# Layer norms of a two-layer hybrid decoder: who sums tiles 5 and 6 of the second token half, and where TensorE's sums stand

## What is computed

```
x <- LN(alpha*x + 0.5*SwiGLU_1(x))
p  = x @ W_in            (attention, short convolution and S5 branches, gates)
x <- LN(alpha*x + W_o( sum_i sigmoid(g_i) * y_i ))
x <- LN(alpha*x + 0.5*SwiGLU_2(x))

LN: mu = mean(x), var = mean((x - mu)^2) over the 1024 features of a token,
    y = (x - mu) / sqrt(var + eps) * g + b
```

## Time and profile before

| | us |
|---|---|
| median of 3 runs | 2511.76 |
| lowest and highest | 2508.62, 2515.42 |
| the profiled execution | 2513.35 |
| its span, first to last instruction | 2511.5 |
| TensorE busy in it | 2488.8 |
| VectorE busy | 1498.5 |
| ScalarE busy | 1056.1 |
| GpSimd busy | 1336.6 |
| mean granted TensorE clock | 0.995 |

### The profile page before, as it was taken

One profiled execution on the slowest core, in us unless ns is written; L12 is line 12 of the kernel. 1 busy time (PEld: TensorE's weight loads), 2 busy tenths in 40 slices (PEclk: granted clock), 3 DMA queues, 4 the chain that ended last, 5 costly groups with the idle time before them and its releaser, 6 DMA issues.

```text
span 2511.5 us, 50783 instructions
## 1 busy us (share of the span) xinstructions
PE 2488.8 (99%) x19996; PEld 2373.0 (94%) x19996; DVE 1498.5 (60%) x2640; ACT 1056.1 (42%) x1934; POOL 1336.6 (53%) x840
## 2 busy tenths in 40 slices
PE   9999999999999999999999999999999999999998
PEld 9999999998899999999999999999977788989897
DVE  7556956975453474535575569569754535836366
ACT  3555234235432253636354542342355322537363
POOL 4767435522244456858557674355222444669582
PEclk9999999999999999999999999999999999999999
DMA  5524323432233323333234242234222333334232
GB/s 146 135 67 106 93 77 94 112 81 66 59 81 89 101 76 101 102 101 107 79 90 135 68 114 85 76 94 112 79 68 58 82 99 97 85 101 118 84 102 84
DMA packets 479750, 232.60 MB, mean 93 GB/s; under 512 B 58960, under 2 KB 479056, under 8 KB 479536
## 3 DMA queue, kind: packets, MB, share of 16 engines
q1 hardware_dynamic: 460288, 220.53, 32.9%
q10 hardware_dynamic: 19248, 9.08, 1.5%
HBM read 220.79 MB, written 4.26 MB: 90 GB/s over the span
## 4 chain that ended last, share of the span: by engine, by line
PE 93%; issue 2%; DVE 2%; POOL 1%; ACT 1%; DMA 1%; ACTq 0%; POOLq 0%; SPq 0%; DVEq 0%
PE ps L760 54%; PE ps L928 24%; PE ps L907 4%; PE ps L785 4%; PE ps L1252 1%; PE ps L1291 1%; POOL w_lo L680 1%; PE ps L833 1%; PE ps L1256 1%; PE ps L1267 1%; PE ps L1174 0%; PE ps L1164 0%; PE ps L1269 0%; PE ps L1101 0%; PE ps L1073 0%
## 5 line engine op out<-in xcount | busy, mean ns | idle before, releaser
L680 POOL TENSOR_TENSOR w_lo<-w_raw,w_hi 128x1024 fp32r<-128x1024 f32 (+3 forms) x348 | 732.1, 2113 | 891.4 <-ACT w_hi L1423 891.0
L1423 ACT ACTIVATE w_hi<-w_raw 128x1024 fp32r<-128x1024 f32 (+3 forms) x348 | 315.6, 911 | 548.1 <-PE ps L760 227.3
L760 PE MATMUL ps<-x_hi,w_hi 128*128 128x264 f32 (+2 forms) x1904 | 288.9, 301 | 0.2
L760 PE MATMUL ps<-x_hi,w_lo 128*128 128x264 f32 (+2 forms) x1904 | 280.0, 296 | 0.6 <-POOL w_lo L680 0.6
L760 PE MATMUL ps<-x_lo,w_hi 128*128 128x264 f32 (+2 forms) x1904 | 280.3, 296 | 0.0
L760 PEld LDWEIGHTS ps<-x_hi,w_hi 128*128 128x128 f32 x1904 | 252.2, 188 | 13.5 <-ACT w_hi L1423 0.6
L680 POOL TENSOR_TENSOR w_lo<-w_pair,w_hi 128x512 fp32r<-128x512 f32 x186 | 246.6, 1340 | 30.9 <-ACT w_hi L1423 30.9
L760 PEld LDWEIGHTS ps<-x_hi,w_lo 128*128 128x128 f32 x1904 | 252.4, 188 | 10.3 <-POOL w_lo L680 1.3
L760 PEld LDWEIGHTS ps<-x_lo,w_hi 128*128 128x128 f32 x1904 | 252.5, 188 | 9.0
L680 POOL TENSOR_TENSOR w_lo<-w_sum,w_hi 128x512 fp32r<-128x512 f32 x155 | 202.6, 1320 | 93.5 <-ACT w_hi L1423 92.0
L760 PE MATMUL ps<-hid_hi,w_hi 128*128 128x264 f32 (+1 forms) x1040 | 161.9, 300 | 0.0
(11 more groups left out here) (349 smaller groups left out, 4912.2 us busy)
## 6 DMA issues: line engine op xcount, KB each, us to landing
w_raw<-in_w_in SPq DMA_DIRECT2D x82, 512.0 KB, 3.9
w_pair<-in_ffn_w_gate SPq DMA_DIRECT2D x64, 512.0 KB, 5.2
w_raw<-in_ffn_w_down SPq DMA_DIRECT2D x64, 512.0 KB, 4.1
w_pair<-in_ffn_w_up SPq DMA_DIRECT2D x60, 512.0 KB, 5.3
w_raw<-in_ffn_w_up SPq DMA_DIRECT2D x28, 512.0 KB, 3.9
w_raw<-in_ffn_w_gate SPq DMA_DIRECT2D x24, 512.0 KB, 3.8
w_raw<-in_ffn_w_down SPq DMA_DIRECT2D x32, 384.0 KB, 3.5
w_raw<-in_w_o SPq DMA_DIRECT2D x16, 512.0 KB, 4.0
```

What stands on the lines that cost most here:

```text
L680: pool.tensor_tensor(held(w_lo, c), src, held(w_hi, c).bitcast(f32), ALU.subtract).then_inc(w_split, 1)
L760: ins = nc.tensor.matmul(dst, wk, x[:, k0 + k, tokens], start=first and k == 0 and n == 0, stop=last and k == n_tiles - 1 and n == 2)
L1423: return nc.scalar.activation(out, in_, f, **kw)
```

## The change

VectorE now adds tiles 5 and 6 of the second half, and their squares, to its running totals: four additions of 128x264 more in each norm. TensorE's sums are those of the total of tiles 0 to 6 (`second_sums`) and of tile 7 (`last_sums`): 12 products, 24 rows, in each norm. In `first_products` nothing stands ahead of chunk 0 any more; the total's sums stand ahead of tile 3, tile 7's ahead of tile 5 (before: tile 7's ahead of tile 4). In the first and the fourth norm, four products of `ones` by `ones` (`keep_busy`) stand between chunk 0 and chunk 1; their output is not used.

```diff
-SUMS_AT = 4
+SUMS_AT = (3, 5)
+FILLER = 4
...
+            def keep_busy(n):
+
+                for _ in range(n):
+                    nc.tensor.matmul(ps[:, 0, 384:384 + P], ones[:], ones[:], start=False, stop=True, skip_group_check=True)
...
-                         between={(0, 0): lambda: second_sums(n, 4, 5), (0, 1): lambda: second_sums(n, 6),
-                                  (SUMS_AT, 0): lambda: second_sums(n, 7)} if n >= 0 else {})
+                         between={(0, 1): lambda: keep_busy(0 if n % 3 else FILLER), (SUMS_AT[0], 0): lambda: second_sums(n),
+                                  (SUMS_AT[1], 0): lambda: last_sums(n)} if n >= 0 else {})
...
-            def second_sums(n, *tiles):
-
-                for k in tiles:
-                    if k == WHOLE:
-                        pe.wait_ge(ln_sums, n * 3 + 4)
-                        token_sums(n, 1, stat[:, 1], 5, True, False)
-                        token_sums(n, 1, stat[:, 2], 7, True, False)
-                        continue
-                    pe.wait_ge(z_half[1], n * 4 + (k + 1))
-                    ins = token_sums(n, 1, z[:, k], 5, False, k == KD - 1)
-                    if k == KD - 1:
-                        ins.then_inc(ln_stat, 1)
-                    pe.wait_ge(ln_square, n * 12 + (k + 5))
-                    ins = token_sums(n, 1, stat[:, square_row(k, 1)], 7, False, k == KD - 1)
-                    if k == KD - 1:
-                        ins.then_inc(ln_stat, 1)
+            def second_sums(n):
+
+                pe.wait_ge(ln_sums, n * 3 + 4)
+                for src, bank in ((stat[:, 1], 5), (stat[:, 2], 7)):
+                    token_sums(n, 1, src, bank, True, False)
+
+            def last_sums(n):
+
+                k = KD - 1
+                pe.wait_ge(z_half[1], n * 4 + (k + 1))
+                token_sums(n, 1, z[:, k], 5, False, True).then_inc(ln_stat, 1)
+                pe.wait_ge(ln_square, n * 12 + (k + 5))
+                token_sums(n, 1, stat[:, 3 + k % 2], 7, False, True).then_inc(ln_stat, 1)
...
-                    if h and k > WHOLE:
+                    if h and k == KD - 1:
                         return
                     total = ps[:, 4 + h, 0:sp.half]
-                    st.done(tt(stat[:, 1, cols] if h or k == KD - 1 else total, total, z[:, k, cols], ADD))
+                    st.done(tt(stat[:, 1, cols] if k == KD - 1 - h else total, total, z[:, k, cols], ADD))
...
                         if h == 0 and k == 0:
-                            add_half_square(WHOLE, 1, 9).then_inc(ln_sums, 1)
+                            st.done(add_half_square(WHOLE, 1, 9))
...
                         if h == 0 and k in TAKES_IN[nk]:
+                            if TAKES_IN[nk][k] == 6:
+                                st.done(add_half_square(5, 1, 10))
                             take_half(TAKES_IN[nk][k], 1)
+                            if TAKES_IN[nk][k] == 7:
+                                add_half_square(6, 1, 11).then_inc(ln_sums, 1)
```

More of the change, by code:

```diff
@@ L439, in edge @@
             return ps[0:EDGE, bank, c0:c0 + min(QT[j][1], 32)]
-        def square_row(k, h):
-            return 0 if (k, h) == (KD - 1, 1) else 3 + k % 2
         def restored(l, which):
@@ L1414, in _ @@
                 ffn(l, 1)
-            second_sums(3 * DEPTH - 1, *range(WHOLE, KD))
+            second_sums(3 * DEPTH - 1)
+            last_sums(3 * DEPTH - 1)
             spread_mean(3 * DEPTH - 1, 1)
@@ L1473, in square @@
                 else:
-                    ins = ACTV(stat[:, square_row(k, h), cols], z[:, k, cols], ACT.Square)
+                    ins = ACTV(stat[:, 3 + k % 2, cols], z[:, k, cols], ACT.Square)
                 ins.then_inc(ln_square, 1)
@@ L1936, in add_half_square @@
                     dve.wait_ge(ln_square, n * 12 + square)
-                    return tt(stat[:, 2, cols] if h or k == KD - 1 else total, total, stat[:, 3 + k % 2, cols], ADD)
+                    return tt(stat[:, 2, cols] if k == KD - 1 - h else total, total, stat[:, 3 + k % 2, cols], ADD)
                 if which == 1:
@@ L2599, in _ @@
                 st.close()
-DVE_STEPS = 396
+DVE_STEPS = 408
 _WEIGHTS = ("ffn1_w_gate", "ffn1_w_up", "ffn1_w_down", "w_in", "mla_w_uq", "mla_w_ukv", "mla_w_o", "conv_w_out",
```

## The result

The changed kernel takes 2531.32 us in the median (2528.66 to 2534.3, 4 runs) against 2512.61 for the one before on the same chip (2508.62 to 2515.42, 4 runs). The ratio is 1.0077, with a 95% interval of 1.006 to 1.0094: **slower by 0.77%**, 18.7 us. The profiled execution took 2533.53 us.

A forecast was written before the change was run, and what follows sets the result against it. TensorE, busy 99%, was taken to bound the kernel, with chunk 1 gated by VectorE. 2507.1 (without clock losses) + 2.6 + 1.7 + 2.2 + 0.2 = 2513.8, plus 14.0 for three clock falls, gave 2527.8 us; range 2511 to 2532.

The forecast's parts named there:

- Chunk 1 is gated by VectorE, and the gate moves back: Chunk 1 waits for VectorE's taking of tile 7; three additions ahead delay it 0.9 us, and TensorE stands still 2.6 us.
- Second and third norm, +1.3 each at full clock: nk = 8 norms: 0.4 us from the later gate and 0.89 of sums now behind it; 2.6 us for two.
- the gate's 0.4: Second and third norm: chunk 1 starts at 902.45 where it started at 902.05.
- Fifth norm, +1.7: The gate binds already, so the whole 0.9 us delay counts, and about 0.8 of sums.
- First and fourth norm, +1.1 each: nk = 6 norms: filler 0.88 us, waits of 1.05 ahead of tile 2 and 0.6 ahead of tile 6; 2.2 for two.
- Last norm, +0.2: Additions lie in VectorE's 1.04 us wait for the last sums and TensorE has fewer sums; bounds -0.5 and +1.
- The clock, three falls at 4.66, 14.0: Second, third and fifth norm: a thinner stretch ahead of chunk 1 drops the clock in each, 4.66 us apiece, 14.0 together.
- the upper price: 4.66 us per fall rather than 1.57, since two groups of sums (total, tile 7) still lie behind the gate.
- No fall in the first and the fourth norm: The filler's 0.88 us of dense products and shorter waits keep the clock up; already in the 2507.1 baseline.
- The rival in which the clock holds: The clock holds despite the gap, 2513.8 us, or falls cost only 1.57 each, 2518.5; chance 0.28 together.
- The faster rival: VectorE's additions vanish in its waits, tile 7 is taken by 899.8 in the second norm, 2500.0 us; chance 0.08.

The follow-up runs named there:

- e1: Changed kernel with eight dense filler products between chunk 0 and chunk 1 in the second, third, fifth and last norm too; 2517.05 us, ratio 1.0023.
- e3: Changed kernel without VectorE's four additions, so TensorE's new order alone (tiles 5 and 6 missing from the second half's sums); 2520.34 us, ratio 1.0034.
- e6: Changed kernel without its own filler in the first and fourth norm (FILLER = 0); 2526.07 us, ratio 1.0063.
- e9: Changed kernel with eight one-column filler products between chunk 0 and chunk 1 in the second, third, fifth and last norm; 2529.78 us, ratio 1.0078.
- e12: Changed kernel with chunk 0's products of tiles 3 and 4 moved ahead of chunk 1 in the nk = 8 norms (lead 5); 2515.02 us, ratio 1.0013.
- e5: Kernel before with four stand-in additions more on VectorE in each norm, both inputs in SBUF; 2521.08 us, ratio 1.0043.
- e7: Kernel before with lead 4 and its sums spread among the products, tile 6's sums kept ahead of chunk 1; 2506.67 us, ratio 0.9987.
- e11: Kernel before with lead 4, sums spread (tile 6's behind chunk 1's tile 1), and four stand-in additions per norm, one input in PSUM; 2528.66 us, ratio 1.0073.
- e8: Kernel before with lead 4, sums spread (tile 6's behind chunk 1's tile 1), and four stand-in additions per norm, both inputs in SBUF; 2533.02 us, ratio 1.0096.
- e10: Kernel before with four stand-in additions more on VectorE in each norm, one input in PSUM; 2513.98 us, ratio 1.0011.

## Why the prediction was right, step by step

The forecast was 2527.8 with a range of 2511 to 2532, and slower at 0.64. The median is 2531.3, inside the range near its upper end, and slower. The mechanism is the one forecast, for the three norms that carry most of the loss. Two sizes were low (the first four norms, the last), and the price of the falls came out right in part by luck.

- **Chunk 1 is gated by VectorE, and the gate moves back.** Shown: the three waits of 2.2 to 2.3 us released by the taking of tile 7, e1, in which chunk 1 starts at the same distance with the gap filled, and e3. The taking of tile 7 came 1.0 us later for 0.9 forecast. Chunk 1 started at 903.51 - 889.68 = 13.83 after the first half's spreading, against 902.05 - 888.86 = 13.19 before: 0.64 for 0.4. The gap is 2.27 us for 2.6, since chunk 0 itself waits 0.80 for tile 6, put at 0.5. From chunk 1 to the spreading of the second mean e1 takes 6.76 us at 1.00 (6.7 forecast) and the change 12.37 at 0.50 (up to 11.5 forecast).
- **Second and third norm, +1.3 each at full clock.** It is 20.59 - 18.99 = 1.6 each (e1's windows): the gate's 0.64 and 0.96 for the sums behind it. The term "the gate's 0.4" was the one put too low.
- **Fifth norm, +1.7:** 20.05 - 18.54 = 1.5.
- **First and fourth norm, +1.1 each:** against before without its falls (18.24 - 1.57 = 16.67), 18.14 is +1.5, of which 0.87 is the filler (e6). Here the waits are 0.70 ahead of tile 2 and 0.48 ahead of tile 6, for 1.05 and 0.6; chunk 0 started at 388.17 for 387.75, since tile 6 was taken 1.1 us later for 0.95.
- **Last norm, +0.2:** mis-sized. 12.43 became 14.52. TensorE waits 2.03 us for the last addition (L1937), and behind that wait its sums ran at the lower clock. In e1, with the same wait, the norm took 12.94, so 0.5 is the order's and 1.6 the clock's. I had let VectorE's own wait of 1.04 us hide the additions and put no clock term there. That term does not come every time: e9 has it (14.43), while e6 and e12, which have this norm as the changed kernel has it, took 12.94 at 1.00.
- **The clock, three falls at 4.66, 14.0:** 5.6 + 3.1 + 5.4 = 14.1. The sum is right; the single prices are not, and that they meet is luck. The third norm has the same two groups of sums behind its gate as the second and paid 3.1, so the reason for taking the upper price, the groups that still had to pass, does not hold. Against e1's lengths the same three falls cost 13.2 us in e9 and 12.1 in e6.
- **No fall in the first and the fourth norm:** right, but "the filler" as its reason is not: e6 has no fall there without it. What keeps the clock there is not told apart by these runs. No gap of 2 us stands ahead of chunk 1, and the sums ahead of both chunks are gone; either could be it.
- **The rival in which the clock holds** (2513.8 to 2518.5) is what e1 and e12 measure once the clock does hold: 2517.1 and 2515.0. So the structural part was sound, if 1 to 3 us low.
- **The faster rival** needed tile 7 taken by 899.8. It was taken by 903.36, which is 902.5 in the timing of the kernel before; 902.4 was forecast.

From 2513.35 in the profiled execution before: -6.2 (its two falls, gone), +8.2 (structure: 2 x 1.5, 2 x 1.6, 1.5, 0.5), +14.1 (clock in three norms), +1.6 (clock in the last) give 2531.0; measured were 2533.5. The other 2.5 us lie between the norms, where the change touches nothing. The span less its six windows is 2403.0 before and 2405.5 after. With e9 and e6, which have the change too, it is 2403.4 and 2402.7, with e1, e3 and e12 2405.0, 2406.6 and 2406.8; without TensorE's new order it lies between 2402.0 and 2405.5 in six traces. In e3, e5 and e12 the clock falls once more between 520 and 530 us, in e1 near 1779. So much of the 2.5 can be scatter, but the traces with the new order are 2 us higher on the average, and what that is stays open.

## What to carry to other kernels

Ahead of a gate that another engine opens, work taken away gave no time here, and taken away from TensorE it cost some: first the stretch went empty, then the clock fell, and what TensorE did for the next 7 to 14 us ran at 0.50. Look for the gate first, then put dense work that has to be done anyway ahead of it (e12), and only if there is none, a filler (e1). A filler where the clock holds without it is pure cost (e6). Sums over partitions with one column did best singly between products that don't wait (e7); where the products waited, that order lost its gain (e11). Of all the kernels here only e7 is faster than the one before, by 0.13%.

## What the runs showed of the hardware

**Eight one-column products did not hold the clock where eight of 128 columns did.** In e9 TensorE was idle for 0.59 us and busy with one-column products for 1.8, and the granted clock fell to 0.50 in the second, third and fifth norm, as in the changed kernel with 2.27 us of idle time. With dense products in the same place, and 0.47 us of idle time, it stayed at 1.00 (e1). The Trainium skill ("TensorE: Matmul & The Clock Gate", "Why this matters for your kernels") names, for drops in mid-kernel, idle gaps alone, and longer ones; by that rule neither kernel would have lost the clock. The measurement decides.

**An addition with both inputs in SBUF took four times as long beside GpSimd.** In e8 the same stand-in takes 1.79 us and, at 388.01, 0.42:

```profile
384.91 1.79 DVE L2009 TENSOR_TENSOR k_rope<-ln_in 128x264 f32<-128x264 f32 x1
...
388.01 0.42 DVE L2009 TENSOR_TENSOR k_rope<-ln_in 128x264 f32<-128x264 f32 x1
...
391.13 1.90 DVE L2009 TENSOR_TENSOR k_rope<-ln_in 128x264 f32<-128x264 f32 x1
```

GpSimd in the same stretch:

```profile
384.01 2.39 POOL L680 TENSOR_TENSOR w_lo<-w_raw,w_hi 128x1024 fp32r<-128x1024 f32 x1 [0.28 <-ACT w_hi L1423]
390.38 2.36 POOL L680 TENSOR_TENSOR w_lo<-w_raw,w_hi 128x1024 fp32r<-128x1024 f32 x1 [3.98 <-ACT w_hi L1423]
```

The long ones begin inside a subtraction of GpSimd (384.01 to 386.40, 390.38 to 392.74) and end 0.3 us behind its end; the short one lies beside none. With one input in PSUM (e10, e11) none is longer than 0.435, though in e11 two of them begin inside such a subtraction as well (385.00 in 384.10 to 386.50, 389.86 in 389.11 to 391.47). The Trainium skill ("GPSIMD Engine Reference", "1. Specifications") says that GpSimd and VectorE share their way to SBUF and collide where an instruction of VectorE has two SBUF inputs; the trace agrees. The changed kernel's additions all read a total in PSUM, and none takes more than 0.442.
